# Second FFN, input projection: seven half-size products per unit instead of eight, with the weight sums made by POOL

## The reference

```python
h = modulate(rms_norm(x, norm_gains[l, 2]), mod[:, 2, 0], mod[:, 2, 1])   # (1 + scale), shift
gate, up = jnp.split(h @ w_in, 2, axis=-1)      # w_in: 1024 x 5632
x = x + 0.5 * mod[:, 2, 2][:, None, :] * ((jax.nn.silu(gate) * up) @ w_down)   # w_down: 2816 x 1024
```

## Time and profile before

| | us |
|---|---|
| Median of 3 runs (lowest, highest) | 1260.99 (1260.57, 1262.89) |
| The profiled execution's own time | 1262.44 |
| Its span on the core | 1260.7 |
| PE busy in it | 1232.3 (98%), 6281 matmuls |
| DVE, ACT, POOL busy | 588.5 (47%), 415.5 (33%), 69.9 (6%) |
| HBM read | 140.65 MB, 113 GB/s over the span |

### The profile page before, as it was taken

One profiled execution on the slowest core, in us unless ns is written; L12 is line 12 of the kernel. 1 busy time (PEld: TensorE's weight loads), 2 busy tenths in 40 slices (PEclk: granted clock), 3 DMA queues, 4 the chain that ended last, 5 costly groups with the idle time before them and its releaser, 6 DMA issues.

```text
span 1260.7 us, 15440 instructions
## 1 busy us (share of the span) xinstructions
PE 1232.3 (98%) x6281; PEld 1022.9 (81%) x6281; DVE 588.5 (47%) x712; ACT 415.5 (33%) x456; POOL 69.9 (6%) x110
## 2 busy tenths in 40 slices
PE   6999999999999999999999999999999999999997
PEld 5788888888789997877887788888988888888887
DVE  5645545545443567566563253355423232332222
ACT  6422221222222456544352422234322222222322
POOL 2000000000000122331220000000000000000000
PEclk9899999999999999999999999999999999999999
DMA  9454565565454121122112233342233223322321
GB/s 354 148 188 160 186 200 154 179 200 158 151 182 144 34 85 53 34 67 67 50 52 68 71 130 100 100 134 68 67 100 100 68 98 100 100 91 65 109 69 67
DMA packets 122288, 143.45 MB, mean 114 GB/s; under 512 B 4084, under 2 KB 102784, under 8 KB 122240
## 3 DMA queue, kind: packets, MB, share of 16 engines
q1 hardware_dynamic: 122032, 142.68, 34.8%
q10 hardware_dynamic: 208, 0.08, 0.0%
HBM read 140.65 MB, written 2.10 MB: 113 GB/s over the span
## 4 chain that ended last, share of the span: by engine, by line
PE 90%; DVE 4%; ACT 3%; issue 1%; DMA 0%; ACTq 0%; DVEq 0%
PE PS L509 27%; PE PS L511 26%; PE PS L510 26%; PE PS L783 4%; PE PS L823 1%; PE PS L552 1%; PE PS L554 1%; PE PS L553 1%; PE PS L665 1%; PE PS L810 1%; PE PS L793 1%; DVE ACC0b L1561 1%; DMA PST<-in_lb_logits_dram 0%; ACT WH L1010 0%; DVE TNH L1470 0%
## 5 line engine op out<-in xcount | busy, mean ns | idle before, releaser
L509 PE MATMUL PS<-HH,WH 128*128 128x512 f32 (+1 forms) x1064 | 418.1, 393 | 4.1 <-DVE HL L1476 2.7
L511 PE MATMUL PS<-HH,WL 128*128 128x512 f32 (+1 forms) x1064 | 407.1, 383 | 0.0
L510 PE MATMUL PS<-HL,WH 128*128 128x512 f32 (+1 forms) x1064 | 406.5, 382 | 0.0
L1430 DVE TENSOR_TENSOR WL<-RAW,WH 128x2048 fp32r<-128x2048 f32 (+2 forms) x93 | 207.7, 2234 | 363.1 <-ACT WH L1010 363.1
L1010 ACT ACTIVATE WH<-RAW 128x2048 fp32r<-128x2048 f32 (+2 forms) x93 | 173.2, 1862 | 384.3 <-PE PS L511 330.9
L509 PEld LDWEIGHTS PS<-HH,WH 128*128 128x128 f32 x1064 | 200.2, 188 | 50.7 <-issue 5.7
L511 PEld LDWEIGHTS PS<-HH,WL 128*128 128x128 f32 x1064 | 200.3, 188 | 45.5
L510 PEld LDWEIGHTS PS<-HL,WH 128*128 128x128 f32 x1064 | 200.5, 188 | 41.3 <-issue 1.1
L509 PE MATMUL PS<-UH,WH 128*128 128x512 f32 (+1 forms) x416 | 148.7, 357 | 0.1
L511 PE MATMUL PS<-UH,WL 128*128 128x512 f32 (+1 forms) x416 | 146.9, 353 | 0.0
L510 PE MATMUL PS<-UL,WH 128*128 128x512 f32 (+1 forms) x416 | 146.7, 353 | 0.0
(11 more groups left out here) (253 smaller groups left out, 1150.7 us busy)
## 6 DMA issues: line engine op xcount, KB each, us to landing
RAW<-in_ffn_w_in_dram SPq DMA_DIRECT2D x42, 1024.0 KB, 5.1
ADAW<-in_w_ada_dram SPq DMA_DIRECT2D x56, 512.0 KB, 5.8
RAW<-in_w_in_mix_dram SPq DMA_DIRECT2D x22, 1024.0 KB, 5.2
RAW<-in_ffn_w_down_dram SPq DMA_DIRECT2D x16, 1024.0 KB, 6.0
ADA<-in_w_ada_dram SPq DMA_DIRECT2D x16, 512.0 KB, 10.8
RAW<-in_ffn_w_down_dram SPq DMA_DIRECT2D x7, 768.0 KB, 4.4
RAW<-in_w_out_dram SPq DMA_DIRECT2D x3, 1024.0 KB, 5.2
XST<-in_x_dram SPq DMA_DIRECT2D x4, 512.0 KB, 5.6
```

Source lines behind the costliest of these rows:

```text
L509: mm(ps, whi, ahi, start=start, stop=False)
L510: mm(ps, whi, alo, start=False, stop=False)
L511: return mm(ps, wlo, ahi, start=False, stop=stop)
L1430: V.tensor_tensor(WL[s][:, 0:size], RAW[s][:, 0:size], WH[s][:, 0:size].bitcast(F32), ALU.subtract)\
```

## The change

For pairs 2 to 10 of the second FFN's input a unit is no longer computed as 2 x 2 x 2 = 8 half-size products (weight quarters of 4 blocks of input x 128 outputs, token quarters of 4 blocks x 256 tokens), which the 48 matmuls amount to, but by Winograd's form of Strassen's scheme, with seven.

- With weight quarters a11, a12, a21, a22 (first index: output block, second: half of the input) POOL makes s1 = a21 + a22, s2 = s1 - a11, s3 = a11 - a21, s4 = a12 - s2, each 128x512, from RAW into SW (`weight_sums`). The order on POOL is s1, s3, s2, s4. s1 waits for the load and until DVE has used s1 and s2 of the unit before, s3 until it has used s3 and s4 (`op_lo`).
- Once, DVE makes from token quarters b11, b12 (first index: half of the input, second: half of the tokens), b21, b22 the sums t1 = b12 - b11, t3 = b22 - b12, t2 = b11 + t3 and b21 - t2 (`token_sums`, 13 instructions), which ACT and DVE split. The split t3 takes the place of b12 in HH and HL, which pair 1 still reads.
- PE's products P1 to P7 of a unit, each 4 blocks x 3 matmuls of 256 columns: a11 b11, s1 t1, s2 t2, a12 b21, s3 t3, s4 b22, a22 (b21 - t2), accumulated in the four banks c11, c12, c21, c22 of the half. Between them ACT copies c11 to c21 ahead of P3 (`seed_p6`, the seed of c21) and c22 to P5 in SBUF (`keep_p5`), DVE adds P5 and c21 into c12 ahead of P5's product (`seed_p5`) and into c22 ahead of P7 (`close_c22`, the closing).
- A unit's operands are split in pieces while PE works on the unit before: s1 and s2 after P3 has freed their place, a11 and a12 (the column blocks) after P4, s3 and s4 after P6, a22 (the last quarter) in a place of its own per half.
- Pair 1 keeps 512 columns but writes banks 4 to 7 (`second_pair`). PE waits for all four token sums after it.
- The products u of pairs 5 to 10 go to UF in float32 and are split after the last unit, since the place of their UH holds TH and TL until then; pairs 2 to 4 are split as before. `down_pair` gets a wait ahead of its second piece.
- The first unit of the down projection is split in two halves, behind P3 and P4 of the last unit.
- SP's program is unchanged. `unit_lo` of pairs 2 to 10 is now raised by the low part of the last quarter, behind all four sums.

```diff
+        UF = place("UF", [P, FB, T], FB * T * 4)
+        UF_FROM = 5
+        TN3 = place("TN3", [P, DB, T], 4096)
+        TS = place("TS", [P, 4, 4, T // 2], 69632)
+        TH = place("TH", [P, 3, 4, T // 2], 2 * UF_FROM * T * 4, F32R)
+        TL = place("TL", [P, 3, 4, T // 2], 2 * UF_FROM * T * 4 + 12288, F32R)
+        SW = place("SW", [P, 4, 4 * P], 98304)
+        P5 = place("P5", [P, 2, T // 2], 94208)
...
+        ROW = slice(HT, T)
+        SEVEN_FROM = 2
+        OP = dict(a11=(1, 0), a12=(1, 1), s1=(1, 2), s2=(1, 3), s3=(0, 0), s4=(0, 1), a22=((0, 2), (0, 3)))
...
+            def weight_sums(n, u, raw_val, after=True):
+
+                quarters = RAW[slot(n)][:, :].rearrange("p (h k m c) -> p h m k c", h=2, m=2, c=P)
+                a11, a12, a21, a22 = quarters[:, 0, 0], quarters[:, 1, 0], quarters[:, 0, 1], quarters[:, 1, 1]
+                s1, s2, s3, s4 = (SW[:, j, :].rearrange("p (k c) -> p k c", c=P) for j in range(4))
+                pool.wait_ge(raw_in[slot(n)], raw_val)
+                if after:
+                    pool.wait_ge(op_lo, 3 * u - 2)
+                nc.gpsimd.tensor_tensor(s1, a21, a22, ALU.add).then_inc(s_made, 1)
+                if after:
+                    pool.wait_ge(op_lo, 3 * u)
+                nc.gpsimd.tensor_tensor(s3, a11, a21, ALU.subtract).then_inc(s_made, 1)
+                pool.wait_ge(s_made, 4 * u + 1)
+                nc.gpsimd.tensor_tensor(s2, s1, a11, ALU.subtract).then_inc(s_made, 1)
+                pool.wait_ge(s_made, 4 * u + 3)
+                nc.gpsimd.tensor_tensor(s4, a12, s2, ALU.subtract).then_inc(s_made, 1)
+
+            first7 = unit_of(SEVEN_FROM, 0)
+            pool.wait_ge(h_lo, 5 * DB)
+            weight_sums(first7, 0, raw_value(first7), after=False)
+            weight_sums(first7 + 1, 1, raw_due(SEVEN_FROM, 1))
+            with pool.Fori(SEVEN_FROM + 1, NP) as i:
+                for half in range(2):
+                    weight_sums(N_F2IN + half, seven(i, half), raw_due(i, half))
...
+                    if piece == 1 and which == 1:
+                        pe.wait_ge(u_lo, 1 + NP + 8)
+                        pe.wait_ge(u_hi, NP + 8)
...
+            def product(bank, op, bhi, blo, start, signal):
+                place_in, at_ = op
+                for k in range(4):
+                    w = slice(4 * P * at_ + P * k, 4 * P * at_ + P * (k + 1))
+                    hi, lo = WH[place_in][:, w], WL[place_in][:, w]
+                    for j, (wt, at_tokens) in enumerate(((hi, bhi), (hi, blo), (lo, bhi))):
+                        ins = mm(PS[:, bank, ROW], wt, at_tokens[:, k, :], start=start and k == 0 and j == 0,
+                                 stop=k == 3 and j == 2, skip_group_check=True)
+                ins.then_inc(signal, 1)
+            def seven_products(i, half):
...
+                if half == 0:
+                    pe.wait_ge(silu_done, 1 + NP + i)
+                else:
+                    pe.wait_ge(umul_done, 1 + NP + i)
+                pe.wait_ge(op_lo, 3 * u + 2)
+                product(c11, OP["a11"], *b11, True, prod)
+                product(c22_, OP["s1"], *t1, True, prod)
+                pe.wait_ge(seed_b, u + 1)
+                product(c21, OP["s2"], *t2, False, prod)
+                product(c11, OP["a12"], *b21, False, prod)
+                pe.wait_ge(op_lo, 3 * u + 3)
+                pe.wait_ge(seed_c, u + 1)
+                product(c21, OP["s3"], *t3, False, prod)
+                product(c12, OP["s4"], *b22, False, prod)
+                pe.wait_ge(unit_lo, unit_of(i, half) + 1)
+                pe.wait_ge(c22, u + 1)
+                product(c21, OP["a22"][half], *t4, False, unit_done)
+
             first_units(N_F2IN, ((0, 1), (2, 3)), 2)
-            swiglu_in(N_F2IN, 1, False, first=1)
-            pe.wait_ge(u_lo, 2 * NP)
-            pe.wait_ge(u_hi, 2 * NP - 1)
+            second_pair()
+            pe.wait_ge(tok_lo, 4)
+            with pe.Fori(SEVEN_FROM, NP) as i:
+                for half in range(2):
+                    seven_products(i, half)
+            pe.wait_ge(u_lo, 1 + NP + UF_FROM)
+            pe.wait_ge(u_hi, NP + UF_FROM)
             pe.wait_ge(silu_done, 1 + 2 * NP)
 
...
+            def token_hi(j):
+
+                act.wait_ge(t_made, (1, 5, 9, 13)[j])
+                if j == 1:
+                    act.wait_ge(unit_done, unit_of(1, 1) + 1)
+                A(quarter_of(HH, 0, 1) if j == 1 else TH[:, (0, None, 1, 2)[j], :, :], TS[:, j, :, :], ACT.Copy)\
+                    .then_inc(tok_hi, 1)
+
+            def silu(i, ps, split):
+                n = unit_of(i, 0)
+                act.wait_ge(unit_done, n + 1)
+                act.wait_ge(umul_done, 1 + NP + i)
+                act.wait_ge(u_lo, 1 + NP + (i if split else UF_FROM))
+                A(SG[:, :, :].rearrange("p m (t c) -> p (m t) c", c=ps.shape[2]), ps, ACT.Silu).then_inc(silu_done, 1)
...
+            def sums_hi(u, j, freed):
+                act.wait_ge(s_made, 4 * u + 3 + j)
+                act.wait_ge(*freed)
+                A(WH[1 - j][:, 8 * P * (1 - j):8 * P * (2 - j)], SW[:, 2 * j:2 * j + 2, :].rearrange("p s c -> p (s c)"),
+                  ACT.Copy).then_inc(op_hi, 1)
...
+            def seed_p6(i, half):
+                u = seven(i, half)
+                act.wait_ge(prod, 6 * u + 1)
+                A(PS[:, 4 * half + 2, ROW], PS[:, 4 * half, ROW], ACT.Copy).then_inc(seed_b, 1)
+
+            def keep_p5(i, half):
+                u = seven(i, half)
+                act.wait_ge(prod, 6 * u + 2)
+                A(P5[:, half, :], PS[:, 4 * half + 3, ROW], ACT.Copy).then_inc(p5_out, 1)
...
+            def seven_ahead(i, half):
+
+                u, nxt = seven(i, half), (i, 1) if half == 0 else (i + 1, 0)
+                due = raw_due(*nxt)
+                n = N_F2IN + nxt[1]
+                last_quarter_hi(n, due, nxt[1], (unit_done, unit_of(i, half) - 1))
+                sums_hi(u + 1, 0, (prod, 6 * u + 3))
+                columns_hi(n, due, (prod, 6 * u + 4))
+                sums_hi(u + 1, 1, (prod, 6 * u + 6))
+
+            act.wait_ge(unit_done, unit_of(0, 0) + 1)
+            act.wait_ge(u_lo, 1 + NP)
+            A(SG[:, :, :], PS[:, 0:2, :], ACT.Silu).then_inc(silu_done, 1)
+            split_hi(unit_of(1, 0), raw_value(unit_of(1, 0)), unit_of(0, 0) + 1)
+            token_hi(0)
+            split_hi(unit_of(1, 1), raw_value(unit_of(1, 1)), unit_of(0, 1) + 1)
+            u_high(0)
+            token_hi(2)
+            token_hi(3)
+            silu(1, PS[:, 4:6, :], True)
+            first7 = unit_of(SEVEN_FROM, 0)
+            sums_hi(0, 0, (unit_done, unit_of(1, 0) + 1))
+            columns_hi(first7, raw_value(first7), (unit_done, unit_of(1, 0) + 1))
+            token_hi(1)
+            seed_p6(2, 0)
+            keep_p5(2, 0)
+            sums_hi(0, 1, (unit_done, unit_of(1, 1) + 1))
+            last_quarter_hi(first7, raw_value(first7), 0, (unit_done, unit_of(1, 1) + 1))
+            u_high(1)
+            seven_ahead(2, 0)
...
+            def up_part(i, split, ahead=True):
+                seed_p6(i, 1)
+                keep_p5(i, 1)
+                silu(i, PS[:, 0:4, ROW], split)
+                if ahead:
+                    seven_ahead(i, 1)
...
+            last7 = seven(NP - 1, 1)
+            n = N_F2DOWN
+            act.wait_ge(raw_in[slot(n)], raw_value(n))
+            act.wait_ge(prod, 6 * last7 + 3)
+            A(WH[slot(n)][:, UNIT // 2:UNIT], RAW[slot(n)][:, UNIT // 2:UNIT], ACT.Copy).then_inc(op_hi, 1)
+            act.wait_ge(prod, 6 * last7 + 4)
+            A(WH[slot(n)][:, 0:UNIT // 2], RAW[slot(n)][:, 0:UNIT // 2], ACT.Copy).then_inc(unit_hi, 1)
+            split_hi(n + 1, raw_value(n + 1), n)
+            for i in range(UF_FROM, NP):
+                act.wait_ge(umul_done, 1 + NP + i + 1)
+                A(UH[:, 2 * i:2 * i + 2, :], UF[:, 2 * i:2 * i + 2, :], ACT.Copy).then_inc(u_hi, 1)
             down(N_F2DOWN, 0, 28, 29, final=True)
...
+                dve.wait_ge(t_ready, 5 * DB)
+                dve.wait_ge(shift_diff, 1)
+                n11, n12, n21, n22 = (quarter_of(TN3, kh, th) for kh, th in ((0, 0), (0, 1), (1, 0), (1, 1)))
+                V.tensor_tensor(TS[:, 0, :, :], n12, n11, ALU.subtract).then_inc(t_made, 1)
+                for k in range(4):
+                    V.scalar_tensor_tensor(TS[:, 1, k, :], n22[:, k, :], SHD[:, k:k + 1], n12[:, k, :], ALU.add, ALU.subtract)\
+                        .then_inc(t_made, 1)
+                for k in range(4):
+                    dve.wait_ge(t_made, 2 + k)
+                    V.scalar_tensor_tensor(TS[:, 2, k, :], n11[:, k, :], sh3[:, k:k + 1], TS[:, 1, k, :], ALU.add, ALU.add)\
+                        .then_inc(t_made, 1)
+                for k in range(4):
+                    dve.wait_ge(t_made, 6 + k)
+                    V.scalar_tensor_tensor(TS[:, 3, k, :], n21[:, k, :], sh3[:, 4 + k:5 + k], TS[:, 2, k, :], ALU.add,
```

(99 more changed lines are left out.)

103 lines of the change are left out of this document (96 added, 7 removed).

## The result

The changed kernel took 1244.94 us (median of 4 runs, 1242.66 to 1250.87), the kernel before beside it 1261.94 (1260.57 to 1266.18): a ratio of 0.9867, 95% interval 0.9823 to 0.991: 1.3% faster, clear of none and under 2%. The forecast was 1247.6, with a range of 1244.0 to 1257.0. The profiled execution took 1246.37 us.

What follows compares the result with a forecast made beforehand. TensorE's (PE's) matmul stream was taken to bound the kernel: 20.16 gained, less 6.0 for the way in and 0.7 for the clock, gives 13.4 us, so 1247.6 us against the median, range 1244 to 1257.

Steps and rivals of the forecast that it cites:

- PE's stream: Units of pairs 2 to 10: 84 matmuls at 0.120 replace 48 at 0.2333, gaining 1.12 a unit, 20.16 us.
- The way in: Behind pair 1: PE idles 2.7 at the start, 1.1 ahead of P5, 1.6 ahead of P7, 0.5 later; together 6.0 us.
- POOL's addition: Each 512-element weight sum takes 1.13 us, upper bound 1.16; in the trace 1.15 to 1.2 alone, up to 2.3 behind DVE.
- a slack of 0.5: Steady units: the round through POOL, DVE and ACT keeps PE's pace of 10.08 us with some 0.5 us to spare.
- the round grows by four times p: Steady unit: any growth in p, the length of one POOL addition, lengthens the 8.8 us (9.9 with u's split) round fourfold.
- A: The main forecast: undisturbed POOL additions, 12 to 15 us faster, 1246 to 1249; chance 0.62.
- B: Rival: POOL's additions take 1.3 to 1.5 us and pace units, leaving 1250 to 1256; chance 0.17.
- The couple: POOL's sums and DVE's low parts, all in SBUF, nearly exclude each other: 0.75 measured per turn, 0.91 by the skill's rule.
- The clock: PE's idle behind pair 1 is followed by a lower clock, costing 0.7 us, bounds 0 and 1.6.
- Cover: Token sums run while DVE sat idle, late conversions of u beside the first down unit: cost 0.
- nothing after 960: Sign in PE's timeline: one idle near 923, two more within 15 us, and no idle after 960.
- C: Rival: POOL's addition above 1.6 us paces all 18 rounds; gain used up at 1.6, 1268 at 1.7; chance 0.11.

Runs made afterwards that it cites:

- pool_short: Changed kernel with POOL adding only 8 of every 128 columns, leaving out most of the weight sums: 1241.18 us, ratio 0.9827 to the kernel before.
- pool_extra: Changed kernel with one more POOL subtraction per unit (s3 made twice): 1260.58 us, ratio 0.9987 to the kernel before.
- again: Changed kernel timed once more without any edit: 1244.74 us, ratio 0.985 to the kernel before.
- early: Changed kernel with PE waiting for the split of the fourth token sum (t3) ahead of P5, not P1: 1244.34 us, ratio 0.985 to the kernel before.
- after_shift: Changed kernel with a second unused 16-byte tile that moves HH and others to 196384: 1248.18 us, ratio 0.9887 to the kernel before.
- before_shift: Kernel before with only the change's 16-byte tile added, unused, moving HH and others up 32 bytes: 1258.2 us, ratio 0.9972 to the kernel before.

## Why the prediction was right, and where its steps were off

**PE's stream**: the form was right (84 matmuls of 256 columns at their own step, not at half of the longer one). The term was too small: 18 x (48 x 0.2333 - 84 x 0.1187) = 22.1, not 20.16. The 0.1200 is the step of the kernel before, read rightly, and did not carry over. On equal places the change is worth 18 x (48 x 0.2324 - 84 x 0.1187) = 21.3. The jump of the loop costs 0, as taken.

**The way in**: forecast 2.7 + 1.1 + 1.6 + 0.5, taken as 6.0 (the terms add to 5.9), measured 2.99 + 1.01 + 1.89 + 0.89 and some 1.0 in small pieces, 7.8. The mechanisms are those named, at the rows named. The first was 0.3 too small: PE starts 0.36 behind DVE's end (923.53 + 1.22 to 925.11), where I took 0.1; behind the two later waits it is 0.15. The second was right, with small copies of 0.37 and 0.39 in place of 0.45. The third and fourth vanish with short additions (pool_short), so it is the addition that was taken too small.

**POOL's addition**: this is the term that was off. I took 1.13 and called 1.16 the bound, twice the 256-element row; it is 1.25, and 1.37 to a dependent one. That row was no bound: in it one of the two inputs is a column that is repeated, where the weight sums read two full ones. The sign "1.15 to 1.2 alone" was wrong, and so was "a slack of 0.5". The rule that the round grows by four times p was right: 4 x 0.12 makes of the forecast's 8.8 and 9.9 the 9.3 and 10.4 that pool_extra points to. Lying between A's 1.13 and B's 1.3, the addition left the circle at PE's pace, with 0.15 a unit to spare at best. "Up to 2.3 when DVE was first" holds (2.28).

**The couple**: I let the measurement of the earlier trace rows stand against the rule of the Trainium skill, "SBUF — State Buffer" (section "SBUF: two separate sides"), that the second of the two waits to the end. The trace bears both out. The low parts of 967.21 and 997.29 wait to POOL's end, as the rule has it, with 0.13 of their 1.22 beside POOL. Where the two take turns, POOL's additions of 906.54 and 908.78 start 2.24 apart, where one split (1.13) and one addition (1.25) make 2.38: 0.14 less, close to the 0.16 of the 256-element couple. So the saving is a fixed one for a turn, small beside long instructions.

**The clock**: 0.7 forecast, 0 measured: 1.00 from 921 to 926, and a mean of 1.00 over the stage in the changed kernel, again and early. after_shift, with the same gap, does have the fall that I took into account (0.66 above), 1.7 us of PE's time and another 1.4 behind it, of which a part fell into waits. Of the six profiles with this gap ahead of P1 five have 1.00 behind it; the forecast's 0.7 was a fair mean of both kinds, not a price that every execution pays.

**Cover**: token sums and late conversions cost nothing, as said. DVE's last token sum ends at 893.9, its next split starts at 897.16. The down stage is 0.7 shorter (128.88 for 129.56), and before_shift has 129.00: most of it goes with the place. Not foreseen were the small restarts behind 960, which the forecast's sign ("nothing after 960") excluded.

**The sum**: in the stage 22.1 - 7.8 = 14.3 (224.00 to 209.66), forecast 13.4. The profiled spans differ by 16.0: 14.3 in the stage, 0.9 ahead of pair 1, 0.7 behind. Against before_shift's 223.08 the stage gained 13.4. So the forecast of what the seven products do was right to 0.1 us, but by luck: its errors cancelled (+1.1 in the steps, -1.8 in the waits, +0.7 in the clock). What it missed, some 3.6 of the 17 us between the medians, goes with the place of the tiles; with that taken off, the median would be near 1248.7, still in the range. No rival came true. POOL's turn with DVE paced three pairs by 0.15 each (20.09 for 19.94), no more, and pool_extra shows how near B and C were: 1.37 more in each round is 0.34 more for each of four additions, 1.59 in place of 1.25, and it uses up the gain (0.9987), where C had it used up at 1.6.
